# Mixer of a two-layer transformer: order of ScalarE's rounding, exponentials and copies, and of the key and value norms, changed

## What is computed

```python
h = rmsnorm(x, norm_mix[l])
qa, ka, va, qb_, kb, vb, qc, kc, vc, gate_logits = jnp.split(h @ w_in[l], split_points, axis=-1)
# A: 8 query heads, 2 key heads, normed per head and rotated
q = axial_rope(rmsnorm(q, qg), rope); k = axial_rope(rmsnorm(k, kg), rope)
y_a = softmax(q k^T / 8) v
# B: windowed, with a bias and a sink in the softmax;  C: two softmaxes, the second weighed by lam
attn = p[:, :, :, 0] - lam * p[:, :, :, 1]
y_c = rmsnorm(attn v, subln_g) * (1 - lambda_init)
branches = einsum(stack(y_a, y_b, y_c), w_branch[l]);  gates = sigmoid(gate_logits)
x = x + sum(gates * branches) @ w_out[l]
```

## Time and profile before

| | us |
|---|---|
| median of 3 runs | 3236.44 (3235.82 to 3241.89) |
| span of the profiled execution | 3231.7 |
| TensorE busy | 2839.8 (88%) |
| VectorE busy | 1155.2 (36%) |
| ScalarE busy | 988.5 (31%) |
| GpSimd busy | 173.0 (5%) |
| first mixer | about 232 to 500 |
| second mixer | about 915 to 1182 |

### The profile page before, as it was taken

How to read it: one execution, slowest core, us unless ns; L and a number is a source line. 1 busy time by engine, 2 the same in 40 slices (tenths; PEclk the granted TensorE clock), 3 DMA queues, 4 the chain that set the end, 5 groups by cost and what they waited for, 6 DMA issues and landing times.

```text
span 3231.7 us, 63044 instructions
## 1 busy us (share of the span) xinstructions
PE 2839.8 (88%) x27834; PEld 1878.6 (58%) x27834; DVE 1155.2 (36%) x1576; ACT 988.5 (31%) x1508; POOL 173.0 (5%) x229
## 2 busy tenths in 40 slices
PE   8999899999998899999989888899888878776665
PEld 6777777778776777765333222345777774433322
DVE  4445555445455555423000000433444434100001
ACT  4435444444344445431100000213444431100000
POOL 0001100000002000000000000002222210000000
PEclk9999999999999999998999999999999998877777
DMA  6463234475652354412799999721000005999997
GB/s 249 175 252 143 102 121 182 173 268 183 237 190 95 115 191 180 169 60 108 306 421 421 422 421 421 323 93 71 10 16 10 10 4 229 390 421 421 421 421 324
DMA packets 100987, 708.62 MB, mean 219 GB/s; under 512 B 11604, under 2 KB 12372, under 8 KB 17280
## 3 DMA queue, kind: packets, MB, share of 16 engines
q1 hardware_dynamic: 92736, 670.80, 52.7%
q10 hardware_dynamic: 7344, 31.45, 2.6%
q0 software_dynamic: 656, 2.52, 0.2%
HBM read 703.65 MB, written 1.07 MB: 218 GB/s over the span
## 4 chain that ended last, share of the span: by engine, by line
PE 64%; DMA 20%; DVE 6%; ACT 5%; issue 3%; POOL 1%; SPq 0%; DVEq 0%; ACTq 0%; POOLq 0%
DMA weight_ring<-in_stream 20%; PE banks L643 8%; PE banks L645 7%; PE banks L644 7%; PE banks L1879 7%; PE banks L1745 3%; PE banks L959 3%; PE banks L2192 3%; PE banks L961 3%; PE banks L960 3%; PE banks L2238 2%; PE banks L2611 1%; PE banks L2598 1%; PE banks L1088 1%; PE banks L1784 1%
## 5 line engine op out<-in xcount | busy, mean ns | idle before, releaser
L1879 PE MATMUL banks<-weight_ring,scratch 128*32 128x256 f32 (+1 forms) x4456 | 602.4, 517 | 179.1 <-DMA weight_ring<-in_stream 157.8
L1879 PEld LDWEIGHTS banks<-weight_ring,scratch 128*32 128x32 f32 (+1 forms) x4456 | 189.6, 130 | 558.9 <-DMA weight_ring<-in_stream 298.9
L640 DVE TENSOR_TENSOR split_high<-weight_ring,split_high 128x1024 fp32r<-128x1024 f32 x198 | 243.4, 1230 | 283.1 <-ACT split_high L635 281.7
L635 ACT CAST split_high<-weight_ring 128x1024 fp32r<-128x1024 f32 x198 | 207.9, 1052 | 313.8 <-PE banks L645 263.5
L1282 DVE TENSOR_TENSOR split_high<-weight_ring,split_high 128x1024 fp32r<-128x1024 f32 x128 | 160.0, 1256 | 201.2 <-ACT split_high L1177 200.8
L2012 DVE TENSOR_TENSOR scratch<-scratch,banks 128x512 f32<-128x512 f32 (+1 forms) x32 | 17.7, 554 | 580.0 <-PE banks L1879 580.0
L2940 ACT COPY scratch<-banks 128x512 f32<-128x512 f32 (+2 forms) x208 | 152.8, 767 | 222.6 <-PE banks L2602 128.8
L643 PE MATMUL banks<-split_high,features_low 128*128 128x512 f32 x528 | 211.0, 400 | 4.0 <-DVE features_low L562 4.0
L645 PE MATMUL banks<-split_high,features_high 128*128 128x512 f32 x528 | 207.5, 393 | 0.0
L644 PE MATMUL banks<-split_high,features_high 128*128 128x512 f32 x528 | 207.2, 392 | 0.0
L959 PE MATMUL banks<-split_high,features_low 128*128 128x512 f32 x416 | 171.1, 411 | 19.5 <-DVE split_high L1282 16.2
(11 more groups left out here) (393 smaller groups left out, 4698.5 us busy)
## 6 DMA issues: line engine op xcount, KB each, us to landing
weight_ring<-in_stream SPq DMA_DIRECT2D x637, 1024.0 KB, 11.3
scratch<-in_kept ACTq DMA_DIRECT2D x11, 1024.0 KB, 20.0
scratch<-in_pair_rows ACTq DMA_DIRECT2D x8, 448.0 KB, 3.6
scratch<-in_lora ACTq DMA_DIRECT2D x2, 1536.0 KB, 17.6
front<-in_gain_rows ACTq DMA_DIRECT2D x5, 512.0 KB, 3.8
bias<-bias_rows POOLq DMA_DIRECT2D x1, 2304.0 KB, 14.5
scratch<-in_routing ACTq DMA_DIRECT2D x2, 1040.5 KB, 5.4
resid<-in_x SPq DMA_DIRECT2D x2, 512.0 KB, 3.8
```

Of the source, the lines that this page charges most:

```text
L635: act.copy(split[i % 4][0], source(i)).then_inc(*self.rounded.up())
L640: dve.tensor_tensor(lo, source(i), hi.bitcast(F32), ALU.subtract).then_inc(*self.rest.up())
L1879: last = pe.matmul(self.psum[q * M:(q + 1) * M, (GATE, UP, DOWN)[part], 0:W], left, w[:, j * D + q * W:j * D + (q + 1) * W], start=(k == 0 ...
```

## The change

- `exps`: ScalarE casts halves up to at_scores+4 (was +3) ahead of the eight exponentials, and none between the fourth and the fifth. `maxima` ends with the low parts up to at_scores+4 (was +5).
- `save_probs`: the halves up to at_probs+2 (was +3) are cast ahead of the copies.
- `square_keys` writes to columns 7168 to 8448 of the arena (`key_squares`) instead of `tmp`, and `mean_keys` reads them there. These columns belong to branch C's gates, which are written later.
- GpSimd waits for the projection (`gated`, 4) and computes the 16 turned parts, waits for the squares, does the four multiplications and the sum, then waits for the inverse and multiplies by it last.
- VectorE: `scale_values` stands ahead of `maxima(2)`.

```diff
--- before.py
+++ after.py
@@ -893,6 +893,7 @@
         a_ss, a_rs, a_ri = (st[:, 64 + i * 20:84 + i * 20] for i in range(3))
         c_ss, c_rs, c_ri = (st[:, 128 + i * 8:136 + i * 8] for i in range(3))
         tmp_c = self.tiles(5120, TT, NB)
+        key_squares = self.tiles(7168, TT, 640)
         bias_placed = self.ge.count
         HALF = CHUNK // 2
         N_HALVES = 64
@@ -1185,11 +1186,9 @@
 
             def exps(ph):
                 branch, at = branch_of[ph], at_scores[ph]
-                to(at + 3)
+                to(at + 4)
                 wait(act, self.maxed, ph + 1)
                 for i in range(8):
-                    if i == 4:
-                        to(at + 5)
                     src = self.psum[:, 4 + i // 2, (i % 2) * SEQ:(i % 2 + 1) * SEQ] if branch == "A" else probs[:, i, :]
                     act.activation(probs[:, i, :], src, ACT.Exp, bias=negm[:, i:i + 1],
                                    scale=0.125 if branch == "A" else 1.0, accum_out=den[:, i:i + 1]).then_inc(*self.expd.up())
@@ -1200,7 +1199,7 @@
                     act.activation(lam2[:, 0:2], lam2[:, 0:2], ACT.Exp).then_inc(*self.sunk.up())
 
             def save_probs(ph):
-                to(at_probs[ph] + 3)
+                to(at_probs[ph] + 2)
                 for g in range(4):
                     wait(act, self.probs_turned, 4 * ph + g + 1)
                     act.copy(probsT[:, 4 * g:4 * g + 4, :], self.psum[:, 4 + g % 2, :].rearrange("p (a b) -> p a b", a=4))\
@@ -1208,7 +1207,7 @@
 
             def square_keys():
                 wait(act, self.gated, 4)
-                act.activation(tmp, proj[:, :, 0:640], ACT.Square).then_inc(*self.squared.up())
+                act.activation(key_squares, proj[:, :, 0:640], ACT.Square).then_inc(*self.squared.up())
 
             def root(n, out, src):
                 wait(act, self.mean_ready, n)
@@ -1309,7 +1308,7 @@
                         dve.tensor_tensor(snk, sink, negm, ALU.add).then_inc(*self.maxed.up())
                     else:
                         dve.tensor_scalar(negm, mx, -1.0, None, ALU.mult).then_inc(*self.maxed.up())
-                to(at_scores[ph] + 5)
+                to(at_scores[ph] + 4)
 
             def outputs(ph):
                 branch, t = branch_of[ph], ph % 2
@@ -1344,7 +1343,7 @@
 
             def mean_keys():
                 wait(dve, self.squared, 1)
-                then(dve.tensor_reduce(a_ss, A[:, 11528:12808].rearrange("p (h c) -> p h c", c=HD), AX.X, ALU.add))
+                then(dve.tensor_reduce(a_ss, A[:, 7168:8448].rearrange("p (h c) -> p h c", c=HD), AX.X, ALU.add))
                 dve.tensor_scalar(a_ss, a_ss, 1.0 / HD, EPS, ALU.mult, ALU.add).then_inc(*self.mean_ready.up())
 
             def invert_keys():
@@ -1389,8 +1388,8 @@
             invert_keys()
             outputs(1)
             norm_values()
+            scale_values()
             maxima(2)
-            scale_values()
             low(0, at_outs["C"], yT_lo, yT_hi, outs_banks["C"])
             outputs(2)
             maxima(3)
@@ -1439,8 +1438,7 @@
                     pool.tensor_tensor(turns[n][:, :, 1, mine:mine + 16], rope[:, :, 1, mine:mine + 16],
                                        g[:, o:o + 16].unsqueeze(1).to_broadcast([P, TT, 16]), ALU.mult).then_inc(*self.ge.up())
             pool.wait_ge(self.ge.sem, self.ge.count)
-            wait(pool, self.inverted, 1)
-            then(pool.tensor_tensor(v, v, bc(a_ri.rearrange("p (t h) -> p t h", t=TT), HD), ALU.mult))
+            wait(pool, self.gated, 4)
             for n, h in ((0, slice(0, 8)), (1, slice(8, 10))):
                 for t in range(TT):
                     heads = h.stop - h.start
@@ -1450,13 +1448,16 @@
                                            turns[n][:, t, 1, mine:mine + 16].unsqueeze(1).to_broadcast([P, heads, 16]), ALU.mult)\
                             .then_inc(*self.ge.up())
             pool.wait_ge(self.ge.sem, self.ge.count)
+            wait(pool, self.squared, 1)
             for n, h in ((0, slice(0, 8)), (1, slice(8, 10))):
                 for t in range(TT):
                     heads = h.stop - h.start
                     pool.tensor_tensor(v[:, t, h, :], v[:, t, h, :], turns[n][:, t, 0, :].unsqueeze(1).to_broadcast([P, heads, HD]),
                                        ALU.mult).then_inc(*self.ge.up())
             pool.wait_ge(self.ge.sem, self.ge.count)
-            pool.tensor_tensor(v, v, w, ALU.add).then_inc(*self.keys_normed.up())
+            then(pool.tensor_tensor(v, v, w, ALU.add))
+            wait(pool, self.inverted, 1)
+            pool.tensor_tensor(v, v, bc(a_ri.rearrange("p (t h) -> p t h", t=TT), HD), ALU.mult).then_inc(*self.keys_normed.up())
 
     MOD = 34064
```

## The result

The changed kernel took 3188.14 us (median of 4 runs, 3181.95 to 3195.15) against 3239.16 for the kernel before (4 runs), a ratio of 0.985 with an interval of 0.984 to 0.987: 51 us faster. The forecast had started from 3236.44, the median of the first three of the four runs before. The profiled execution has a span of 3180.2 us against 3231.7, 51.5 less.

A forecast was written before the change was run, and what follows sets the result against it. TensorE and the handovers that make it wait bound the mixers. Lost time saved, 14.5 + 15.9, and half clock, 5.6 + 2.4, total 38.4 us: 3236.4 - 38.4 = 3198 us, range 3190 to 3207.

The forecast's parts named there:

- What bounds a mixer: Both mixers: TensorE, busy nine tenths, and the handovers that make it wait bound them, not the weight stream.
- the two prices of the prediction: TensorE's idles in the mixers: 0.27 us extra for each idle, and 1.6 us for each fall to half clock.
- the sum: TensorE's lost time in the mixers: 14.5 us saved in the first, 15.9 in the second, half clock apart.
- The clock: Half clock after idles: 5.6 and 2.4 us saved; phase 1 still charged one fall per mixer, scores(2) half of one.
- The phases, one by one: Copies of turned probabilities in six attention phases: still six waits, 10.3 us lost per mixer where they were 11.1.
- the save of the keys: Turned keys' save in ScalarE's queue, late behind the second root: scores(2) waits anew, 3.1 us lost, 2.8 idle.
- The port: VectorE and GpSimd shutting each other out beside maxima(1) in phase 1: between 0 and 3.9 us, taken as 1.0.
- Rival (a): GpSimd's sum blocks VectorE's TENSOR_SCALAR of maxima(1), 1.9 us more per mixer, more half clock: saved about 25, 3211; chance 0.12.
- The table load: ScalarE in phase 1 and ahead of scores(2): 1.28 us each, no drain of about 1.4 us added.
- Rival (b): Mixers: handovers shorter, the clock never falls, scores(2) hidden by 1 us more; saved 45 us, 3191; chance 0.11.
- What follows the mixers: Stages behind the mixers: start earlier by what the mixers save, with no saving of their own.
- rival (d): ScalarE becomes the bound, copies later in every phase; slower beyond 3.2 us a phase, 3270 at 6 us; chance 0.02.

The follow-up runs named there:

- all but the keys: The changed kernel with GpSimd's order and the squares for the keys as before, the other parts kept: 3198.88 us, ratio 0.988 to the kernel before.
- the keys alone: The kernel before with only the keys rotated first and normed last, squares in columns of their own: 3235.95 us, ratio 1.000.
- the second profile: The changed kernel measured and profiled once more, nothing changed: 3185.38 us (2 runs), ratio 0.984 to the kernel before.
- the four kernels with fewer casts or filled waits: The changed kernel with one cast less ahead of copies (3191.80 us), that plus turned keys saved earlier (3191.29), unread products in waits (3195.94), cast less plus products (3188.53).
- the filled one: The changed kernel with products that nobody reads put into TensorE's waits ahead of scores(2) and the copies: 3195.94 us, ratio 0.988 to the kernel before.

## Why the prediction was right, and where it fell short

**What bounds a mixer** was right: TensorE and its handovers. Of the 43.8 us in the mixers all can be booked to the two prices of the prediction, within 0.2 us in each mixer. Idle fell from 24.7 and 26.1 us to 11.4 and 11.6; with 0.27 for each of twelve waits before and seven after, that is 14.6 and 15.9 us, against 14.5 and 15.9 in the sum. The clock gave 8.3 and 5.0 us (five and three falls before, none after). 14.6 + 15.9 + 8.3 + 5.0 = 43.8. (The table above starts from waits that are not rounded, hence its 30.8 and 13.4.)

**The phases, one by one.** The idles forecast and measured were 0.9 and 0.90 (phase 0), 3.2 and 2.67 (phase 1; 2.80 in the second mixer), 1.6 and 1.88, 0.7 and 0.82, 0.6 and 0.64, 1.5 and 1.51, and 2.8 and 3.02 at scores(2). That the earlier half is paid for at the copies, and that the save of the keys is late next, was right.

**The port** was sized at 1.0 us in phase 1 and cost 0.3 to 0.5: the kernel with all but the keys has no GpSimd work beside maxima(1) and waits 2.34 us in phase 1 of both mixers, the changed one 2.67 and 2.80. In the first mixer the rows show 0.14 at the TENSOR_SCALAR and 0.2 at the low part ahead of it. What a meeting costs depends on what it hits: the kernel with the keys alone paid 1.6 us for the same work, because a low part with a waiting TensorE behind it was shut out. Rival (a) had the mechanism, but its 1.9 us at the TENSOR_SCALAR came in neither kernel (0.31 us here, 0.17 with the keys alone).

**The table load** needed no drain: 303.35 + 1.28 = 304.63, root at 304.64, and at scores(2) 320.90 + 1.28 = 322.18, evacuation at 322.20. The idle there was 3.0 us, forecast at 2.8. The Trainium skill (ScalarE: Activation LUTs, section What ACT_TABLE_LOAD costs) has a drain of about 1.4 us on top of each load; by an estimate with that figure the idle would have been near 4.2, and the rows do not bear it out.

**The clock is the mis-sized term.** The prediction kept three falls in the mixers after the change and took back 8.0 us; the profile had none and gave 13.3. Rival (b), held at 0.11, had this half right (no fall) and the other wrong: scores(2) was not hidden any better. That there was no fall at all was in part luck, as the second profile with its one fall shows. The reading that idles of 2.6 to 2.8 us go either way was right; of the four such places two were charged as sure and two at half. Fourteen profiles of the two mixers give a better count. These are TensorE's idles by length, and how many of them had a fall that began during the idle or within 3.6 us of its end: 1.2 to 1.8 us, 74 and none; 1.8 to 1.95, 50 and 26; 1.95 to 2.6, 16 and 14; 2.6 to 3.1, 48 and 22; 3.1 to 4, 4 and 2; over 4, 12 and 12. The idles of 1.57 and 1.93 us at the borders are among them. The left group is the changed kernel's three profiles and those of the four kernels with fewer casts or filled waits. Split like this, the length of an idle is not all that counts:

| idle, us | with the whole change, 7 profiles: idles, falls | without it, 7 profiles: idles, falls |
|---|---|---|
| 1.2 to 1.8 | 20, 0 | 54, 0 |
| 1.8 to 1.95 | 22, 5 | 28, 21 |
| 1.95 to 2.6 | 0, 0 | 16, 14 |
| 2.6 to 3.1 | 18, 3 | 30, 19 |
| 3.1 to 4 | 2, 2 | 2, 0 |
| over 4 | 0, 0 | 12, 12 |

With the whole change the clock fell less often behind idles of one length. That does not make the fewer waits around them the cause: in the changed kernel's own three profiles the surroundings are the same each time, and of twelve idles of 2.6 to 3.1 us one had a fall, scores(2) in one mixer, and the same idle in five other places had none. What differed is when the idle came. In each of the fourteen profiles all falls begin on one regular beat, within 0.01 us, from the first to the last, and where the beat starts differs from one execution to the next. How the idles from 1.7 us up lie against that beat separates those with a fall from those without to within 0.02 us, and it does so in the same way in the kernels with and without the change. This is read from the traces; no run moved an idle on purpose. It also means that idles of one profile are not independent draws. The prediction priced each idle by its length alone, from one profile of the kernel before, and that is the step that failed.

**What follows the mixers** was carried over unchanged, and that was the second miss, 7.7 us: 38.4 + 5.3 of the clock in the mixers + 7.7 make up the 51.5 of the profiles but for 0.1. Of it 3.4 us are the fall of the clock behind the idle of 1.93 us at the start of each feed-forward part, which came twice in the profile before and not at all in the one after; 1.9 lie ahead of the first mixer, where nothing differs. The rest is some 2.4. It is a balance of larger parts: the first 465 us behind the second mixer took 464.9 us in the profile before and 458.2 in the one after, and half of TensorE's busy time at half clock in them was 17.5 and 9.9 us; later stages gave some of it back. In size the rest is inside what profiles of unchanged code show: behind the second mixer the kernel before read 2046.2 and 2057.5 us, the changed one 2042.4, 2039.0 and 2042.5, and others up to 2053.4. Medians over 4 to 10 runs carry this with them. The saving of 49 to 51 us in the medians is therefore some 41 to 44 us of mixers and a remainder that goes in part with the clock and whose cause stays open; so does that of the 8 to 11 us between the changed kernel and the filled one.

**Slower** (rival (d)) had no support: the copies' waits stayed below 3 us.

## What to carry to other kernels

Follow each phase from one anchor and write down the queue of the engine that hands over, instruction by instruction: idles came out within 0.3 us in six of seven places, the new one included. Price a part of a change both alone and on top of the others, and split what it gives: the keys' order was worth nothing alone and 12 us at the end, but 6.4 and 5.2 us in handovers, and the rest was the half clock. And count the half clock behind a wait as a cost of its own, which one profile does not settle: between 1.8 and 3.1 us of idle it came or not, for the same idle of the same kernel; none of 74 idles from 1.2 to 1.8 us was followed by a fall, and all 12 over 4 us were. A kernel whose waits lie in the range between has to be profiled more than once before a difference of a few us is read from it.

## What was not expected of the hardware

VectorE and GpSimd shut each other out for whole instructions: a low part of 1.22 us took 2.90 and 2.86 beside GpSimd's norm and sum, and GpSimd's parts of 0.45 took 1.43 beside a low part. Sixteen products of 64x256 and the halves after them ran at a clock of 0.50 behind one idle of 3.00 us and at 1.00 behind another of 3.02. The falls of one execution all begin on one beat, to 0.01 us, which lies elsewhere in the next execution. Filling TensorE's idle with unread products cost nothing in the stage (248.6 us with and without them), and no idle above 1.2 us was left within it.
